# First attention layer: values and gate of each head as one product of seven blocks, with the gate applied ahead of the transposes

## What is computed

```python
hproj = x @ w_in                                  # 512 x 1024 by 1024 x 6144
q, k = rope(q), rope(k) * 256 ** -0.5             # a head: q and k 256 wide, v and gate 512 wide
scores = (q @ k.T) * decay                        # causal, gamma_h ** (n - m)
o = scores @ v
o = (o - mean(o)) * rsqrt(var(o) + 1e-5)          # over the 512 values of a head
y = (o * silu(gate)) @ w_out
x = layer_norm(ALPHA * x + y)
```

## Time and profile before

| | us |
|---|---|
| median of 3 runs | 1416.28 |
| lowest and highest | 1415.32, 1417.46 |
| span of the profiled execution | 1415.9 |
| PE busy | 1395.8 |
| DVE busy | 915.0 |
| ACT busy | 700.6 |
| POOL busy | 388.5 |

### The profile page before, as it was taken

One profiled execution on the slowest core, in us unless ns is written; L12 is line 12 of the kernel. 1 busy time (PEld: TensorE's weight loads), 2 busy tenths in 40 slices (PEclk: granted clock), 3 DMA queues, 4 the chain that ended last, 5 costly groups with the idle time before them and its releaser, 6 DMA issues.

```text
span 1415.9 us, 19394 instructions
## 1 busy us (share of the span) xinstructions
PE 1395.8 (99%) x7444; PEld 1206.5 (85%) x7444; DVE 915.0 (65%) x1546; ACT 700.6 (49%) x1131; POOL 388.5 (27%) x192
## 2 busy tenths in 40 slices
PE   9999999999999999999999999999999899999998
PEld 7888888888889888888888888778888899998887
DVE  6444354549952755545544469946877878789896
ACT  4323232236554533443443356558956465666554
POOL 5334253441034433343334230035304100000000
PEclk9999999999999999999999999999999999999999
DMA  7267946947433987965796557353122576445552
GB/s 291 90 200 201 293 152 171 266 104 267 178 117 122 300 229 215 309 167 161 205 299 161 163 187 293 144 193 125 63 82 75 161 185 173 125 176 211 200 186 111
DMA packets 53890, 260.26 MB, mean 184 GB/s; under 512 B 5568, under 2 KB 10304, under 8 KB 28224
## 3 DMA queue, kind: packets, MB, share of 16 engines
q1 hardware_dynamic: 37152, 163.04, 33.0%
q0 software_dynamic: 5760, 41.95, 15.0%
q10 hardware_dynamic: 10912, 54.40, 11.3%
HBM read 252.03 MB, written 91.23 MB: 242 GB/s over the span
## 4 chain that ended last, share of the span: by engine, by line
PE 86%; DVE 8%; ACT 2%; DMA 2%; POOL 1%; issue 1%; SPq 0%; DVEq 0%; ACTq 0%; POOLq 0%
PE bank L566 23%; PE bank L568 23%; PE bank L567 23%; PE bank L1164 6%; PE bank L1126 4%; PE bank L1226 3%; PE bank L1143 1%; DVE wlo L2070 1%; DMA v_spill<-v_tok 1%; DMA stage<-in_w 1%; DVE wlo_a L2070 1%; POOL wlo L723 1%; DVE br_lo L2070 1%; PE bank L912 0%; PE bank L1306 0%
## 5 line engine op out<-in xcount | busy, mean ns | idle before, releaser
L723 POOL TENSOR_TENSOR wlo<-stage,whi 128x1024 fp32r<-128x1024 f32 (+2 forms) x116 | 291.7, 2538 | 547.3 <-ACT whi L1446 547.3
L1446 ACT ACTIVATE whi<-stage 128x1024 fp32r<-128x1024 f32 (+2 forms) x120 | 122.3, 1070 | 84.1 <-PE bank L568 63.7
L566 PE MATMUL bank<-xhi,whi 128*128 128x512 f32 (+1 forms) x428 | 149.4, 349 | 3.7 <-DVE xlo L2070 1.8
L568 PE MATMUL bank<-xhi,wlo 128*128 128x512 f32 (+1 forms) x428 | 148.5, 347 | 0.0
L567 PE MATMUL bank<-xlo,whi 128*128 128x512 f32 (+1 forms) x428 | 148.3, 346 | 0.0
L1449 ACT ACTIVATE whi<-stage 128x1024 fp32r<-128x1024 f32 (+2 forms) x125 | 118.2, 991 | 38.7 <-PE bank L568 29.3
L2070 DVE TENSOR_TENSOR wlo<-stage,whi 128x1024 fp32r<-128x1024 f32 x108 | 123.8, 1173 | 14.7 <-ACT whi L1449 14.7
L566 PEld LDWEIGHTS bank<-xhi,whi 128*128 128x128 f32 x428 | 81.1, 189 | 14.3 <-issue 2.2
L566 PE MATMUL bank<-whi,xhi 128*128 128x512 f32 (+1 forms) x236 | 91.0, 386 | 1.6 <-POOL wlo L723 1.6
L568 PE MATMUL bank<-whi,xlo 128*128 128x512 f32 (+1 forms) x236 | 90.1, 382 | 0.0
L567 PE MATMUL bank<-wlo,xhi 128*128 128x512 f32 (+1 forms) x236 | 90.1, 382 | 0.0
(11 more groups left out here) (447 smaller groups left out, 3973.0 us busy)
## 6 DMA issues: line engine op xcount, KB each, us to landing
stage<-in_w SPq DMA_DIRECT2D x79, 1024.0 KB, 4.9
tsum<-in_w ACTq DMA_DIRECT2D x32, 1024.0 KB, 14.3
stage<-tsum SPq DMA_DIRECT2D x32, 1024.0 KB, 4.8
tsum<-in_w POOLq DMA_DIRECT2D x16, 1024.0 KB, 10.2
tsum<-tsum POOLq DMA_DIRECT2D x16, 1024.0 KB, 10.3
stage<-in_w SPq DMA_DIRECT2D x8, 1152.0 KB, 7.4
usum<-in_w POOLq DMA_DIRECT2D x8, 1024.0 KB, 9.8
stage<-usum SPq DMA_DIRECT2D x32, 256.0 KB, 3.8
```

Of the source, the lines that this page charges most:

```text
L566: pe.matmul(dst, a_hi, b_hi, start=start, stop=False)
L568: return pe.matmul(dst, a_lo, b_hi, start=False, stop=stop)
L723: pool.tensor_tensor(lo[:, r], stage[p % 2][:, r], hi[:, r].bitcast(F32), ALU.subtract).then_inc(w_lo, 1)
L1446: act.activation(parts(p)[0][:, r], stage[p % 2][:, r], ACT.Copy).then_inc(w_hi, 1)
```

## The change

The weights of a head's values V and gate G are taken as a matrix of 2 x 2 blocks: B11 and B21 are the upper and lower 512 rows of V, B12 and B22 those of G; the tokens likewise (A11 and so on, 256 tokens x 512 rows). Their product is made of seven block products P2 to P8 (the number is the index of the panel in the head; 0 and 1 are q and k).

- **Weights.** Four blocks are loaded per head (1 MB each). DVE makes four sums of them, each 2048 columns wide: T1 = B12 - B11, T3 = B22 - B12, T2 = B22 - T1, T4 = B21 - T2. A head has nine panels to split in place of six. POOL makes the remainders of 0, 1, 2, 6 and 7 (q, k, B11, B22, B21), DVE those of 3, 4, 5 and 8 (T1, T2, T3, T4). A third stage lies in `oT[12:16]`, which is written last.
- **Tokens.** Four sums of token blocks are made once, in head 0, by DVE from x transposed (`xres`), with a rounding by ACT and a remainder by DVE each (`operand_sum`, `vs_a`, `vs_b`). x itself is therefore loaded after the last head.
- **Results.** P7 and P8 are added onto P2 and the scores' bank of P5 in PSUM; DVE puts the others together with ten additions of 512 columns, in `grow` (kept1) and in `gate`.
- **Gate.** It comes out with tokens on the partitions, so that it is applied by the norm itself: DVE makes (o - mean) x gate, ACT scales by the deviation, PE transposes, and ACT copies to `oT`.
- **Order.** The heads are written out on every engine. PE starts the next head's q product ahead of the transposes. The last head's transposes stand behind the first two steps of the output product.

The diff, cut to its core:

```diff
+SPLITS = 9
+A_PANEL = (0, 1, 2, None, None, None, 5, 3, None)
+BY_POOL = {0: 0, 1: 1, 2: 2, 6: 3, 7: 4}
+BY_DVE = {3: 0, 4: 1, 5: 2, 8: 3}
+S_ORDER = (3, 2, 1, 0)
...
+        a_stage = (stage[0][:, 0:PAN], stage[1][:, 0:PAN], oT[:, 12:16, :].rearrange("p a n -> p (a n)"))
+        A_STAGE = (0, 1, 2, 2, 2, 1, 0, 1, 2)
+        kept1 = grow[:, :].rearrange("p (a n) -> p a n", a=2)
+        xt_k = xres[:, :, :].rearrange("p t (a n) -> p (t a) n", a=2)
...
+        def a_operand(j):
+            h, t = slice(0, HALF), slice(HALF, SEQ)
+            return {2: (xhi[:, 0:4, h], xlo[:, 0:4, h]), 3: (vs_a[:, 0, 0], vs_a[:, 0, 1]),
+                    4: (vs_a[:, 1, 0], vs_a[:, 1, 1]), 5: (vs_b[:, 0, 0], vs_b[:, 0, 1]),
+                    6: (vs_b[:, 1, 0], vs_b[:, 1, 1]), 7: (xhi[:, 4:8, h], xlo[:, 4:8, h]),
+                    8: (xhi[:, 4:8, t], xlo[:, 4:8, t])}[j]
...
+            for h in range(HA):
+                if h:
+                    sp.wait_ge(g_plo, 10 * h - 2)
+                    head_load(h, 0)
+                    sp.wait_ge(g_plo, 10 * h)
+                    sp.wait_ge(g_sum, 3 + 4 * h)
+                head_load(h, 1)
+                if h:
+                    sp.wait_ge(g_dlo, 8 * h)
+                head_load(h, 2)
+                if h == 0:
+                    sp.dma_start(rope_a[:, :, :], t["rope_a"]).then_inc(aux["const"], 16)
+                    sp.dma_start(ident[:, :], t["ident"]).then_inc(aux["const"], 16)
+                    sp.dma_start(cols[:, :], t["cols"]).then_inc(aux["const"], 16)
+                sp.wait_ge(g_plo, 10 * h + 2)
+                head_load(h, 6)
+                sp.wait_ge(g_plo, 10 * h + 4)
+                head_load(h, 3)
+                sp.wait_ge(g_dlo, 8 * h + 6)
+                head_load(h, 7)
...
+            at = 0
+            for h in range(HA):
+                for j in BY_POOL:
+                    if (h, j) == (0, 0):
+                        continue
+                    head_lo(h, j)
+                    at += 1
+                    if 6 <= at < 10 or 11 <= at < 15:
+                        sum_step(AO, at - 6 if at < 10 else at - 7, (4, 8), 0)
+                    elif 16 <= at < 20:
+                        up_sum(0, at - 16)
...
+            def head(h):
+                pe.wait_ge(a_q32, 4 * h + 2)
+                block_product(h, 2, X)
+                if h == 0:
+                    pe.wait_ge(vs_l, 1)
+                else:
+                    pe.wait_ge(a_ot, 4 * h)
+                block_product(h, 3, Z)
                 pe.wait_ge(a_qklo, 4 * h + 4)
+                for kt in S_ORDER:
                     for d in range(2):
                         r = slice(kt * P, (kt + 1) * P)
+                        to = (W + Y)[kt][:, 0:SEQ - kt * P]
+                        last = split_dots(pe, to, qk_hi[:, 2 + d, r], qk_lo[:, 2 + d, r],
                                           qk_hi[:, d, kt * P:], qk_lo[:, d, kt * P:], d == 0, d == 1)
                     last.then_inc(a_s, 1)
+                pe.wait_ge(a_dec, 4 * h + 2)
+                if h == 0:
+                    pe.wait_ge(vs_l, 2)
+                block_product(h, 4, Y)
+                pe.wait_ge(a_dec, 4 * h + 4)
+                if h == 0:
+                    pe.wait_ge(vs_l, 3)
+                block_product(h, 5, W)
+                pe.wait_ge(a_c, 10 * h + 4)
+                if h == 0:
+                    pe.wait_ge(vs_l, 4)
+                block_product(h, 6, Z)
+                pe.wait_ge(a_k1, 2 * h + 2)
+                block_product(h, 7, X, True)
+                pe.wait_ge(a_c, 10 * h + 6)
+                block_product(h, 8, W, True)
...
+            for h in range(HA):
+                head(h)
+                if h + 1 < HA:
+                    turned_product(h + 1, 0)
+                    turn_head(h)
+                    turned_product(h + 1, 1)
             for d in range(13):
                 f, g = divmod(d, AO.dq)
+                if d == 2:
+                    turn_head(HA - 1)
...
+                rope(h, 0)
+                rope_lo(h, 0)
+                if h == 0:
+                    operand_sum(0)
+                    operand_sum(1)
+                    operand_sum_lo(0)
+                    dve.wait_ge(vs_s, 1)
+                    operand_sum(2)
+                dve.wait_ge(a_ld[1], 48 * h + 32)
+                dve.wait_ge(g_plo, 10 * h + 6)
+                dve.tensor_tensor(s0, s1, s0, ALU.subtract).then_inc(g_sum, 1)
+                dve.wait_ge(a_ld[0], 32 * h + 32)
+                dve.tensor_tensor(s1, s2, s1, ALU.subtract).then_inc(g_sum, 1)
+                dve.wait_ge(g_sum, 3 + 4 * h + 1)
+                for b in range(2):
+                    head_lo(h, 3, b)
+                if h == 0:
+                    operand_sum_lo(1)
+                    dve.wait_ge(vs_s, 3)
+                    operand_sum(3)
+                rope(h, 1)
+                rope_lo(h, 1)
+                if h == 0:
+                    operand_sum_lo(2)
+                dve.tensor_tensor(s0, s2, s0, ALU.subtract).then_inc(g_sum, 1)
                 dve.wait_ge(aux["decay"], 16 * h + 16)
                 dve.wait_ge(a_qklo, 4 * h + 4)
+                decays(h, 0)
+                decays(h, 1)
+                dve.wait_ge(g_sum, 3 + 4 * h + 3)
+                head_lo(h, 4, 0)
+                decays(h, 2)
+                head_lo(h, 4, 1)
+                decays(h, 3)
+                for b in range(2):
+                    head_lo(h, 5, b)
+                if h == 0:
+                    operand_sum_lo(3)
+                for i, kt in enumerate(S_ORDER):
                     w = SEQ - kt * P
+                    dve.wait_ge(a_shi, 4 * h + i + 1)
                     lo_of(s_lo[:, KT_AT[kt]:KT_AT[kt] + w], work[:, kt, 0:w], s_hi[:, KT_AT[kt]:KT_AT[kt] + w], a_slo)
+                dve.wait_ge(a_k1, 2 * h + 2)
+                dve.wait_ge(a_m, 7 * h + 3)
+                for a in range(2):
+                    dve.tensor_tensor(kept1[:, a, :], kept1[:, a, :], Y[a][:, :], ALU.add).then_inc(a_c, 1)
+                for a in range(2):
+                    dve.wait_ge(a_c, 10 * h + a + 1)
+                    dve.tensor_tensor(gate[:, a, :], kept1[:, a, :], Z[a][:, :], ALU.add).then_inc(a_c, 1)
+                dve.wait_ge(a_ld[1], 48 * h + 48)
+                dve.tensor_tensor(s0, s1, s0, ALU.subtract).then_inc(g_sum, 1)
+                dve.wait_ge(a_m, 7 * h + 4)
+                for a in range(2):
+                    dve.wait_ge(a_c, 10 * h + a + 3)
+                    dve.tensor_tensor(gate[:, 2 + a, :], gate[:, a, :], W[a][:, :], ALU.add).then_inc(a_c, 1)
+                gates(2, 0)
+                gates(3, 1)
+                dve.wait_ge(a_m, 7 * h + 5)
+                for a in range(2):
+                    dve.tensor_tensor(gate[:, a, :], gate[:, a, :], Z[a][:, :], ALU.add).then_inc(a_c, 1)
+                dve.wait_ge(g_sum, 3 + 4 * h + 4)
+                for b in range(2):
+                    head_lo(h, 8, b)
+                gates(0, 2)
+                gates(1, 3)
+                for q in range(2):
+                    v_low(q, X[q][:, :])
+                dve.wait_ge(a_m, 7 * h + 7)
+                for a in range(2):
+                    dve.tensor_tensor(kept1[:, a, :], kept1[:, a, :], W[a][:, :], ALU.add).then_inc(a_c, 1)
+                for q in range(2, TT):
+                    dve.wait_ge(a_c, 10 * h + 7 + q)
+                    v_low(q, kept1[:, q - 2, :])
+                if h == HA - 1:
+                    combine(AO, 2)
...
+                dve.reciprocal(small[:, 2, 0:TT], small[:, 1, 0:TT])
+                dve.wait_ge(a_gt, 4 * h + 4)
                 for q in range(TT):
+                    dve.scalar_tensor_tensor(out=onorm[:, q, :], in0=B[q][:, :], scalar=mv[:, q, 0:1],
+                                             in1=gate[:, q, :], op0=ALU.subtract, op1=ALU.mult).then_inc(a_on, 1)
...
+                for q in range(TT):
+                    act.wait_ge(a_on, 4 * h + q + 1)
+                    copy(onorm[:, q, :], onorm[:, q, :], a_sc, small[:, 2, q:q + 1])
+            def turned_out(h):
+                for j in range(VT):
+                    act.wait_ge(a_t, 4 * h + j + 1)
+                    copy(oT[:, 4 * h + j, :], B[j][:, :], a_ot)
             for h in range(HA):
+                head(h)
                 if h == 0:
                     copy_blocks(AO, 0, 2)
+            act.dma_start(xres[:, :, :], t["x"]).then_inc(aux["x"], 16)
```

412 lines of the change are left out of this document (243 added, 169 removed).

## The result

| | kernel before | changed kernel |
|---|---|---|
| time, median | 1416.78 us (4 runs, 1415.32 to 1417.46) | 1423.91 us (4 runs, 1422.48 to 1424.64) |
| span of the profiled execution | 1415.9 us | 1420.7 us (time 1422.48) |
| matmuls | 7444 | 7348 |
| PE busy in the span | 99% | 97% |

The change is slower: ratio 1.0046, 95% interval 1.0031 to 1.0060, 7.1 us between the medians and 4.8 between the profiled executions. 1415.4 was forecast, with no difference as the likeliest case. 1423.9 lies at the very end of the range, and its side is wrong.

The account below looks back on a forecast made before the run. PE alone was taken to set the time. Terms: -21.8 PE's work, +9.8 head 0, +4.6 head 1, +1.5 heads 1 to 3, +5.0 into the output product = -0.9, so 1415.4 us; range 1407 to 1424.

Parts of the forecast that it names:

- PE's work: All heads: 24 fewer matmuls of 512 columns per head, 96 in all, at 0.2267 us each: 21.8 us less.
- Head 0: DVE is full with added operand work, so PE waits before P3, the scores, P4 and later panels: 9.8 us (7 to 12).
- Head 1: POOL's wait for ACT's four copies stands one panel earlier, delaying P2, P3, scores and P4: 4.6 us (2.4 to 7.4).
- Head 2: Like heads 1 and 3, all waits hidden by slack except at P7 and P8: 0.5 us (0.2 to 0.8).
- nothing late in heads 2 and 3: A condition of the faster rival, 1407 us, chance 0.27: all but P7 and P8 has slack in these heads.
- P6 to P8 in heads 1 to 3: P6 2.8 us early; P7 and P8 late through POOL's halves and DMA issue: 0.5 us a head, 1.5 together.
- Into the output product: Two new PE waits behind the last head, (a) and (b): together 5.0 us, where there was no wait before.
- (a): From P8 to the output product's first operand and remainder takes 7.6 us against 6.8 of inner products: 0.9 with a handoff.
- (b): Output product's third step: x is loaded after the last head and DVE's remainder waits for it: 4.1 us (2.4 to 5.5).
- rival 3: PE's clock falls behind four waits of 2.6 to 4.1 us, 2 us each, 8 more: 1424 us, chance 0.07.
- After that DVE needs 4.6 a step, PE 5.44: Output product behind its third step: DVE needs 4.6 us a step against PE's 5.44.
- The rivals' times: Fewer waits 1407 us (chance 0.27), DVE bound in every head 1422 (0.14), clock falls 1424 (0.07); saving absent (0.02).

Follow-up runs that it names:

- block sums spaced: Changed kernel with POOL's accumulating DMAs for the output product's weights issued with room between, ACT's four head 2 copies behind its rounding for P7: 1418.54 us, ratio 1.0002.

## Why the prediction was wrong, step by step

- **PE's work**: right. 96 matmuls are gone, and where nothing is late the T's stand 72.5 to 72.6 us apart (block sums spaced), 5.2 us a head less than before, of 5.44.
- **Head 0**: right in kind, 8.3 for 9.8. P3 2.70 (3.4), scores 1.07 (3.2, but 1.8 us of slow clock stood in front of them), P4 1.76 (2.2), P6 to P8 0.2 (1.0). That it is DVE's amount of operand work is shown by leaving it out (8.0 us) and by putting it in another order (0.5).
- **Head 1**: the four waits came where they were put and as large: P2 0.45 (0.5), P3 2.36 (2.6), scores 0.46 (0.7), P4 0.62 (0.8), behind POOL's wait for ACT's copies. Their removal with that wait shows the cause.
- **Head 2** is the step that failed, 4.0 of the 6.5 us by which the waits came out larger. "Head 1, a queue that is moved" followed the four copies issued after head 0 and the one wait on POOL. The same queue has a second group, issued at head 1's end, and ACT itself waits for it at head 2's start. Neither that wait nor what stands behind it on ACT was counted, and "nothing late in heads 2 and 3" was listed as speaking for the gain. The landing time was taken from copies that had the queues nearly alone; with POOL's sums one block later, they overlap, and it is 26.8 us. Moving the DMAs takes head 2's loss to nearly nothing, and it does so while such a copy still takes up to 23.7 us (block sums spaced): what counts is who waits for it. ACT's wait and POOL's were moved together, so their shares in head 2 are not told apart.
- **P6 to P8 in heads 1 to 3**: 1.2 us a head, not 0.5. With POOL's DMA issue no longer between the remainders of P6 and P7 it is 0.3, so the issue is most of it; P6's own second half, 0.2 late, had been put down as 2.8 early.
- **Into the output product**: (a) 0.9 as forecast, (b) 4.33 against 4.1, through the chain that was laid out. (x could not have been loaded much earlier than P6 of the last head, since the third and fourth operand lie in its place; the prediction named only x transposed.)
- **The clock**: rival 3 was right in kind and too dear. Filling the waits with matmuls brings the full clock back, so idling is the cause. Of the four waits two were followed by a fall (2.70 and 4.33), the others (scores 1.07, head 1's P3 2.36) not; the slow stretch in head 0 was free, since DVE set the next start, and the other cost 1.4 to 1.5 us, not 2 each. "No slice shows a fall" was right, but the trace before does have one, behind 1.99 and 1.22 us, in stretches shorter than a slice: the trace did bear the rival out. It had a chance of 0.07 with its price at 8; as a term of 1 to 2 us it belonged in the sum.
- **"After that DVE needs 4.6 a step, PE 5.44"** left out DVE's evictions. This did not move the forecast but what one could win from it: x earlier gives 6.1 at the third step and 2 to 4.7 in the end.
- **The rivals' times** are rounded against their own sums: 1407.8, 1422.6 and 1423.4 by these, where 1407, 1422 and 1424 stand. Nothing hangs on it.
- **The frame of the sum**: all four runs of the changed kernel lie 1.74 to 1.82 us above their spans. 0.4 was taken for the kernel before by setting its profiled span, 1415.9, beside the median; by the same 1.8 that execution took 1417.7 us, a little more than any of the four timed ones (to 1417.46). That is why the medians differ by 7.1 and the traces by 4.8. The profiled execution's own time is not known, so this is worked out, not shown.

In sum: the working gave -0.9; 4.0 for head 2, 1.2 for head 1 and 0.8 for head 3 (nearly all P6 to P8), 0.5 and 1.5 at the third step, less 1.5 in head 0, and less 0.9 of gaps of the kernel before, make 4.7.

## What to carry to other kernels

Where a change moves a wait on a queue, follow every group of that queue to its end, the ones a head later too, and price a landing by what else the queues carry then. A wait taken away is worth only what the next engine in line has to spare: read its busy time in that stretch first. A saving in the bounding engine's work that hands 23 us a head to the next engine should come with a plan for the head in which that engine is full.

## What the runs showed of the hardware that was not expected

- An accumulating DMA of 1 MB on POOL's queue holds back the issue of the next one until it has landed (issues 0.2 to 0.3 us behind landings 13.0, 15.5 and 9.1 us after the issue before): POOL stood 7.3 to 12.3 us in such issues in one kernel and up to 14.6 in another, and what was queued behind stood too.
- Copies of 1 MB within HBM, 6.4 to 16.0 us to land before, took up to 26.8 us with accumulating DMAs under way; a load of 1 MB to SBUF, 4.8 us in the median before, took 11.1 beside four such copies and 12.65 beside an accumulating DMA and SP's other loads.
- A DVE operation with both inputs in SBUF waits for POOL's half in progress, however short it is itself: 128 columns took 1.66 us on average, and four such operations in a row each paid.
- In all these kernels up to the second layer's start, the granted clock fell to 0.50 for some 3 to 7 us behind every wait of PE of 3.45 us and more (up to 12.20), and behind none of 1.77 us and less. Between those both were seen: a fall behind 1.99 (one kernel), 2.07, 2.11 and 2.30 (nine remainders on POOL), 2.35 and 2.36 (three kernels), 2.70 and 2.71, and none behind 2.10, 2.36 (changed kernel), 2.69, 2.70, 2.98 and 3.36 us. The two waits at the transposes of x, 1.51 or 1.60 and then 1.98 or 1.99 us, 6 us apart, were followed by a fall in one of three kernels. The length of the last wait alone does not tell.
